# Transposing queries and decay logits before the sigmoids in a fused attention and recurrence kernel

## The reference, cut to what matters

```python
qa, ka, va, za, qr, fr, ir, zr = _project(_rmsnorm(hp, norm_g[l]), w_in[l])
...
log_f = jnp.logaddexp(jnp.log(lb), jnp.log1p(-lb) + jax.nn.log_sigmoid(fpre))
key = (1.0 - lb) * jax.nn.sigmoid(-fpre)
q = jax.nn.silu(qr.astype(f32))
...
cum = jnp.cumsum(log_f, axis=2)
...
scores = jnp.einsum('bhtsd,bhsd->bhts', decay * q[:, :, :, None, :], k)
o = jnp.einsum('bhts,bhsv->bhtv', scores, v) + jnp.einsum('bhtd,bhdv->bhtv', q * jnp.exp(cum), state)
...
o = o_attention * silu(za), o_recurrence * silu(zr), then mix @ w_out and a last rmsnorm
```

## Time and profile before

| | |
|---|---|
| runs | 1533.69, 1535.79, 1536.41 us: median 1535.79 |
| profiled execution | 1534.05 us, of which the span from first to last instruction is 1532.3 |
| PE busy | 1485.4 us, 97% of the span |
| DVE, ACT, POOL busy | 59%, 60%, 51% |
| granted clock of TensorE | 0.993 of full over the span |
| DMA | 30.9% of the 16 engines in the main queue |

### The profile page before, as it was taken

How to read it: one execution, slowest core, us unless ns; L and a number is a source line. 1 busy time by engine, 2 the same in 40 slices (tenths; PEclk the granted TensorE clock), 3 DMA queues, 4 the chain that set the end, 5 groups by cost and what they waited for, 6 DMA issues and landing times.

```text
span 1532.3 us, 25316 instructions
## 1 busy us (share of the span) xinstructions
PE 1485.4 (97%) x8296; PEld 1271.3 (83%) x8296; DVE 901.3 (59%) x2055; ACT 917.5 (60%) x2326; POOL 777.6 (51%) x1492
## 2 busy tenths in 40 slices
PE   5899999997999999999999999999999999999997
PEld 3788888886888888888888888888888888888886
DVE  5566666676555665675565656765556666632332
ACT  6677777684656666676666665866666666611111
POOL 7755655667555665476546565565544435500000
PEclk9999999999999999999999999999999999999999
DMA  8453333251542211224342221124322210244331
GB/s 261 157 182 145 124 124 114 73 150 50 149 128 90 77 60 49 69 67 126 108 126 69 70 70 44 64 72 162 126 71 70 69 67 23 99 142 147 123 123 68
DMA packets 101879, 157.50 MB, mean 103 GB/s; under 512 B 10688, under 2 KB 80192, under 8 KB 93056
## 3 DMA queue, kind: packets, MB, share of 16 engines
q1 hardware_dynamic: 101760, 156.01, 30.9%
HBM read 111.42 MB, written 44.56 MB: 102 GB/s over the span
## 4 chain that ended last, share of the span: by engine, by line
PE 86%; DVE 4%; POOL 4%; issue 2%; ACT 2%; SPq 1%; DMA 0%; POOLq 0%; DVEq 0%; ACTq 0%
PE pab L571 43%; PE oar L638 8%; PE qkb L689 7%; PE qkb L595 6%; PE qkb L753 6%; PE pab L753 6%; PE tb L629 4%; DVE scores L1155 2%; PE tb L668 2%; PE tb L740 1%; POOL w_raw L1318 1%; PE oar L611 1%; PE oar L608 1%; SPq L320 1%; PE oar L610 1%
## 5 line engine op out<-in xcount | busy, mean ns | idle before, releaser
L571 PE MATMUL pab<-w_hi,xr 128*128 128x512 f32 x2176 | 782.8, 402 | 11.7 <-ACT w_hi L809 7.9
L571 PEld LDWEIGHTS pab<-w_hi,xr 128*128 128x128 f32 x2176 | 412.0, 189 | 91.8 <-issue 9.7
L571 PE MATMUL pab<-w_lo,xr 128*128 128x512 f32 x1088 | 426.8, 392 | 0.0
L1383 POOL TENSOR_TENSOR dd<-dd 128x64 f32<-128x64 f32 x340 | 101.5, 298 | 399.1 <-DVE dd L1138 399.0
L571 PEld LDWEIGHTS pab<-w_lo,xr 128*128 128x128 f32 x1088 | 206.8, 190 | 32.7
L689 PE MATMUL qkb<-kp,q 128*128 128x512 f32 (+3 forms) x656 | 184.1, 362 | 2.9 <-DVE mxs L1155 1.6
L860 ACT ACTIVATE fb<-pab,nrs 128x256 f32<-128x256 f32 x68 | 32.2, 474 | 243.3 <-PE pab L571 243.3
L915 ACT ACTIVATE scores<-scores,nmx 128x128 f32<-128x128 f32 (+16 forms) x136 | 156.7, 1161 | 10.1 <-DVE nmx L1165 10.1
L1106 DVE TENSOR_TENSOR q<-tb,q 128x256 fp32r<-128x256 f32 x68 | 28.8, 424 | 225.5 <-ACT kp L902 225.5
L1155 DVE CUSTOM_DVE_ANT_0 scores<-qkb,bias 128x512 f32<-128x512 f32 (+4 forms) x136 | 84.9, 625 | 128.9 <-PE qkb L689 128.8
L638 PE MATMUL oar<-vv,at 128*128 128x128 f32 x1104 | 151.8, 277 | 0.3
(11 more groups left out here) (154 smaller groups left out, 2661.7 us busy)
## 6 DMA issues: line engine op xcount, KB each, us to landing
xr<-xs SPq DMA_DIRECT2D x51, 1024.0 KB, 5.2
xs<-xr SPq DMA_DIRECT2D x17, 1024.0 KB, 4.9
w_raw<-in_w_in SPq DMA_DIRECT2D x48, 256.0 KB, 6.0
w_raw<-in_x_turned SPq DMA_DIRECT2D x17, 512.0 KB, 4.5
mix<-mx SPq DMA_DIRECT2D x68, 128.0 KB, 2.2
xr<-mix SPq DMA_DIRECT2D x17, 512.0 KB, 4.9
w_raw<-in_x_prompt SPq DMA_DIRECT2D x16, 512.0 KB, 3.8
scores<-in_x_prompt SPq DMA_DIRECT2D x16, 512.0 KB, 4.2
```

The source lines that it names most:

```text
L571: last = mm(pab[:, b, :], x, w[:, kt, 512 * b:512 * b + 512], start=(kt == 0 and part == 0 and w is w_hi), stop=(kt == KT - 1 and part == 1))
L1383: g.tensor_tensor(o[:, :, 0, :], ref, c[:, :, 0, :], sub)
```

## The change

- PE transposes the plain recurrent query and decay logits (two transposes out of a new tile rq) ahead of step b = 0, kt = 2 instead of three transposed results ahead of kt = 6.
- ACT's `recurrence_columns` only copies the four column groups; a new `recurrence_sigmoids`, right behind it, makes the sigmoids from the transposed tile in PSUM, so it waits for the transposes. `copy_recurrence` becomes `log_decay` with one instruction.
- DVE makes qt out of the transposed query and the sigmoid; the factor 1 - lb of the key goes into its product with the decays.
- Levels are packed: at the five upper levels only the 64 later columns are made by POOL (in five instructions more), multiplied on PE (128x64 matmuls), masked and added (five adds in place of one reduction). The sum lands in the first 128 columns of masked, of which st is now a view.
- The weights of head 1, half b = 0, are scaled by norm_g while ACT and DVE split them; POOL's eight scalings of them in round 16 of head 0 are gone.

```diff
-                    if b == 0 and kt == 6:
+                    if b == 0 and kt == 2:
                         transpose_recurrence(h, t, first)
...
+                    if part == 0:
+                        mm(qkb[:, u % 2, 0:P], kl[:, 1, :], ql[:, 0:P], start=True, stop=True)
+                    for i, j in enumerate(levels):
+                        c0 = HP * i + (P if part == 0 else 0)
+                        late = 2 * P + HP * j
+                        last = mm(qkb[:, u % 2, c0:c0 + HP], kl[:, 2 + j, :], ql[:, late:late + HP], start=True, stop=True)
...
-                need(pe, h, "pb_free", t + 1)
-                tr(tb[:, u % 2, 0:P], nb[:, :], ident[:, :])
-                tr(tb[:, u % 2, P:2 * P], rc[:, 1, :], ident[:, :])
-                tr(tb[:, u % 2, 2 * P:3 * P], rc[:, 2, :], ident[:, :]).then_inc(S["rect_t"], 1)
+                need(pe, h, "rec_nat", t + 1)
+                for j in range(2):
+                    last = tr(tb[:, u % 2, P * j:P * j + P], rq[:, j, :], ident[:, :])
+                last.then_inc(S["rect_t"], 1)
...
+            def recurrence_sigmoids(h, t):
+                u = rec_use(h, t)
+                need(act, h, "rect_t", t + 1)
+                F(fb[:, 0:2, :].rearrange("p g c -> p (g c)"), tb[:, u % 2, 0:2 * P], ACT.Exp, scale=-1.0)
+                link(h, F(fb[:, 2, :], tb[:, u % 2, P:2 * P], ACT.Exp))
                 link(h, F(fb[:, :, :], fb[:, :, :], ACT.Ln, bias=1.0))
...
+                F(rc[:, :, :], fb[:, :, :], ACT.Exp, scale=-1.0).then_inc(S["rec_sig"], 1)
...
                     recurrence_columns(h, t)
+                    recurrence_sigmoids(h, t)
...
-                    copy_recurrence(h, t)
+                    log_decay(h, t)
...
+                    tt(masked[:, a:b], qkb[:, u % 2, 0:b - a], causal[:, a:b], ALU.mult).then_inc(S["qk_free"], 1)
+                    need(dve, h, "qk_free", u + 1)
+                    for j in levels:
+                        late = st.rearrange("p (b a r) -> p b a r", a=2, r=HALVES[j])[:, :, 1, :]
+                        level = masked[:, P + HP * j:P + HP * j + HP].rearrange("p (b r) -> p b r", r=HALVES[j])
+                        if added:
+                            need(dve, h, "level_sum", (len(HALVES) - 1) * t + added)
+                        summed = tt(late, late, level, ALU.add)
...
-                        if first:
-                            for kt in range(KT):
-                                scale_weights(h, 0, kt)
                         split_weights(h, 1, range(KT))
```

More of the change, by code:

```diff
@@ L93, in scaled_of @@
     if h == 1:
-        return (0 if b else KT) + kt + 1
-    return 2 * KT * (h - 1) + 2 * kt + (1 if b else 2)
+        return kt + 1
+    return KT + 2 * KT * (h - 2) + 2 * kt + (1 if b else 2)
 def hi_of(b, kt):
@@ L589, in rec_scores @@
                 need(pe, h, "q_decayed", t + 1)
-                for part, blocks in enumerate((range(1, 5), range(5, NS))):
+                for part, levels in enumerate(((0, 1), (2, 3, 4))):
                     u = qk_use["rec", t, part]
                     need(pe, h, "qk_free", u - 1)
[L593 to L596, removed]
+                    if part == 0:
[4 more added lines that the diff above has]
+                        last = mm(qkb[:, u % 2, c0:c0 + HP], kl[:, 2 + j, :], ql[:, late:late + HP], start=True, stop=True)
+                    last.then_inc(S["kscore_done"], 1)
                 need(pe, h, "fin_done", t)
@@ L807, in split_weights @@
                         act.wait_ge(S[f"raw_in{b}{kt}"], (h + 1) * 16 + 16)
-                    gain = gn[:, kt:kt + 1] if first else 1.0
+                    gain = gn[:, kt:kt + 1] if h + 1 < HEADS and not scaled else 1.0
                     F(w_hi[:, kt, 512 * b:512 * b + 512], raw_piece(h + 1, b, kt), ACT.Copy, scale=gain
@@ L858, in recurrence_columns @@
                 pb = pab[:, 1, :]
-                scale, minus = xrs[:, t:t + 1], nrs[:, t:t + 1]
-                F(fb[:, 0:2, :].rearrange("p g c -> p (g c)"), pb[:, 0:2 * P], ACT.Exp, scale=minus)
-                link(h, F(fb[:, 2, :], pb[:, P:2 * P], ACT.Exp, scale=scale))
-                link(h, F(fb[:, :, :], fb[:, :, :], ACT.Ln, bias=1.0))
[L863 to L867, removed]
+                F(rq[:, :, :].rearrange("p g c -> p (g c)"), pb[:, 0:2 * P], ACT.Copy, scale=xrs[:, t:t + 1]).then_inc(S["rec_nat"], 1)
+                F(vr[:, slot3(t), :], pb[:, 2 * P:3 * P], ACT.Copy, scale=xrs[:, t:t + 1])
+                need(act, h, "gates", t)
+                F(zz[:, 1, :], pb[:, 3 * P:4 * P], ACT.Copy, scale=xrs[:, t:t + 1])
+                F(ez[:, 1, :], pb[:, 3 * P:4 * P], ACT.Exp, scale=nrs[:, t:t + 1]).then_inc(S["b_evac"], 1)
+            def recurrence_sigmoids(h, t):
[3 more added lines that the diff above has]
+                link(h, F(fb[:, 2, :], tb[:, u % 2, P:2 * P], ACT.Exp))
+                link(h, F(fb[:, :, :], fb[:, :, :], ACT.Ln, bias=1.0))
+                if t > 0 or not (isinstance(h, int) and h == 0):
+                    need(act, h, "k_decayed", t)
+                F(rc[:, :, :], fb[:, :, :], ACT.Exp, scale=-1.0).then_inc(S["rec_sig"], 1)
             def gate_sigmoids(h, t):
@@ L887, in sum_squares, with log_decay @@
                 F(junk[:, P:2 * P], oar[:, 1, 0:P], ACT.Square, accum_out=ssq[:, 1:2]).then_inc(S["sumsq"], 1)
[L889 to L894, removed]
+            def log_decay(h, t):
+                need(act, h, "rec_floor", t + 1)
+                F(lf[:, :], rc[:, 1, :], ACT.Ln, scale=lbh[:, 1:2], bias=lbh[:, 0:1]).then_inc(S["log_f"], 1)
             def copy_qk(h, t):
@@ L1044, in _ @@
             for j in range(2):
-                v.tensor_tensor_reduce(out=nb[:, HD * j:HD * j + HD], in0=lamv[:, 2 * j, :], in1=lamv[:, 2 * j + 1, :], scale=1.0,
+                v.tensor_tensor_reduce(out=rq[:, 0, HD * j:HD * j + HD], in0=lamv[:, 2 * j, :], in1=lamv[:, 2 * j + 1, :], scale=1.0,
                                        scalar=0.0, op0=ALU.mult, op1=ALU.add, accum_out=lam[:, j:j + 1]
@@ L1361, in apply_decay @@
                 need(pool, h, "decay_ready", t + 1)
-                g.tensor_tensor(ql[:, :, :], qt[:, :].unsqueeze(1).to_broadcast([P, NS, P]), xx[:, NX - NS:NX, :],
-                                ALU.mult).then_inc(S["q_decayed"], 1)
+                g.tensor_tensor(ql[:, 0:2 * P].rearrange("p (l c) -> p l c", l=2),
+                                qt[:, :].unsqueeze(1).to_broadcast([P, 2, P]), xx[:, NX - 2:NX, :], ALU.mult)
+                for j, s in enumerate(HALVES):
+                    late = 2 * P + HP * j
+                    halves = [a.rearrange("p (b a r) -> p b a r", a=2, r=s)[:, :, 1, :] for a in (qt[:, :], xx[:, 2 + j, :])]
+                    last = g.tensor_tensor(ql[:, late:late + HP].rearrange("p (b r) -> p b r", r=s), *halves, ALU.mult)
+                last.then_inc(S["q_decayed"], 1)
             def head_scales(h, t, body):
```

86 lines of the change are left out of this document (44 added, 42 removed).

## The result

The changed kernel takes 1555.41 us (median of 4 runs, 1554.02 to 1556.34); the kernel before, run on the same chip, takes 1535.72 (4 runs). The ratio on record is 1.0135, 95% interval 1.0123 to 1.0146 (the two medians alone give 1.0128): slower by 1.3%. The forecast was 1553.0. The profiled execution has a span of 1554.5 against 1532.3 before, so the traces differ by 22.2 us, 2.5 more than the medians: the profiled run of the changed kernel was its slowest.

The account below looks back on a forecast made before the run. PE, busy 97% of the span, bounds the kernel, with the ACT, DVE, combine chain just under it. +30 + 3.3 + 0 - 11 - 5 = +17 on 1534.05 gives 1551, on the median's footing 1553 us; range 1530 to 1573.

Parts of the forecast that it names:

- Long rounds, +30: Rounds 9 to 16: softmax waits behind sigmoids, so PE waits for combine; 7.6 us a head, 30 for four heads.
- Short rounds, 0: Rounds 1 to 8: DVE sets the pace and eats PE's saved transpose; 0 a head, bounds -0.9 and +4.
- First rounds of heads 1 to 3, +3.3: Sigmoids come behind the gate column that waits for POOL; 1.1 us each, 3.3 together.
- Border of heads 0 and 1, -11: POOL's eight scalings go, ending PE's wait ahead of head 1's first recurrent scores; about 11 us gained, bounds 8 and 12.
- Start, -5: Fewer, narrower POOL masks come about 4 us sooner, PE stops earlier for first columns; 5 us gained, range 1 to 6.
- The forecast's +17: Whole kernel: sum of all terms, +30 + 3.3 + 0 - 11 - 5, added to the profiled execution's 1534.05 us.
- slow adds: Rival on DVE's five dependent adds: at 0.35 each, rounds 1 to 8 pay 0.5 each, 16 more, 1569 us; chance 0.12.
- Columns do not set the pace: Denies the rival that matmul width sets PE's pace: 0.56 a round off, at most 4 us gained, 1549; chance 0.05.
- The rule that the prediction weighed: PE's score matmuls: spacing is columns over 2.4 GHz plus 2.5 ns, saving 0.27 a round; prediction went by measured rows.
- The chain stays under PE: Faster rival: long rounds do not wait because the chain stays within PE's 5.94 us; 1512 us if none waits; chance 0.17.
- the 0.14 us here: Round 15 before the change: slack of PE's first softmax-weight transpose after the earliest start that combine allows, 0.14 us.

Follow-up runs that it names:

- The order run: Changed kernel with softmax ahead of the sigmoids in ACT's queue in rounds 9 to 16, transposes unmoved, DVE's columns and decay logarithm moved along: 1534.79 us, ratio 1.0004.
- the three places of the transposes: Changed kernel with only the two transposes moved: to kt = 3, 1735.8 us; to kt = 1, 1537.55 us; to kt = 0 in rounds 9 to 16, 1523.28 us.
- norm_g alone: Kernel before with only head 1's first half of weights multiplied by norm_g in the split, POOL's eight scalings gone: 1523.6 us, ratio 0.993.
- the runs with the late gates: Gates' column copies put behind the softmax: on the changed kernel 1553.32 us; on the one with early transposes in rounds 9 to 16, 1520.77 us.
- two parts of this one: Kernel before with norm_g in one split and the packed levels, without the turned layout: 1518.86 us, ratio 0.99.
- the run with the late transposes: Changed kernel with the two transposes at kt = 3 instead of kt = 2, so behind the recurrent scores too: 1735.8 us, ratio 1.1312.

## Why the prediction came out

Its steps, one by one, with what the trace of the changed kernel gives.

- *Long rounds, +30.* Right in mechanism and size. From the first transpose to PE's L634 the chain is 969.85 to 977.08, 7.23 (worked out: 7.28); the softmax starts 1.99 behind the transpose (2.02). The rounds 9 to 15 lose 6.4 to 6.7 a head (6.1), round 16 of head 1 loses 1.46 (1.5). Four heads: 26.2, and 4 times 1.5, that is 32; the round 16 of the heads 0 and 3 can't be read alone, since the border and the last stage follow them. The order run shows that the queue is the cause, and the three places of the transposes that it is the time of the sigmoids that counts.
- *Short rounds, 0.* Slightly too pessimistic. In round 6 of head 3 of the changed kernel, against the earlier trace rows:

```profile
1114.61 0.38 PE L665 MATMUL tb<-ident,rq 128*128 128x128 f32 x2
...
1120.34 0.82 PE L634 MATMUL tb<-ident,scores 128*128 128x128 f32 x6
...
1116.72 0.23 DVE L1133 TENSOR_SCALAR rc<-rc 128x128 f32<-128x128 f32 x1 [2.76 <-ACT rc L879]
1117.06 0.41 DVE L1101 TENSOR_TENSOR masked<-qkb,causal 128x256 f32<-128x256 f32 x1
...
1119.41 1.15 DVE L1196 SCALAR_TENSOR_TENSOR scores<-scores,cneg 128x512 f32<-128x512 f32 x2
```

  The floor starts 2.11 after the transpose (2.15). From the mask to `combine` it takes 2.35, where 2.05 for the sums and 0.44 for the two small instructions had been taken. So PE keeps the saved transpose: rounds 1 to 8 of heads 1 to 3 win 1.25 each, 3.7 together, a little outside the bound of 0.9 a head.
- *First rounds of heads 1 to 3, +3.3.* 1.03 in head 2, 0.58 in head 3, and some 0.7 in head 1: 2.3.
- *Border of heads 0 and 1, -11.* Rounds 16 and 0 together get 8.8 shorter; with the 1.46 and 0.7 that the points above put on them the gain is 10.9. The scores of head 1's first round follow without a wait. norm_g alone gives 10.5.
- *Start, -5.* **This term was mis-sized.** Round 2 of head 0 begins at 61.5 instead of 62.1: 0.6, under the bound of 1. The masks took 7.25 us, 2.4 less than 9.65, where 4 less had been taken (last section). And PE stops longer for the first columns, 8.6 in the list of waits; the kernel before had, in its list:

```profile
PE tb L659 <- DVE nb L1118: 6.2, 1, 6.2
```

  In the profiled runs of kernels with the same first rounds this point scatters from 59.6 to 62.1, so the term's true size stays open by some 2 us. And what is won there is asked back: in rounds 2 and 3 of head 0 the sigmoids, behind the gates' copies, wait for POOL, +1.4 together, which the runs with the late gates take away (15.25 and 15.63). That scatters too: in the order run, with the same first rounds, these two take 15.25 and 15.66, and round 4 pays instead, 17.33 for 16.39. The prediction had seen that wait in the first rounds of heads alone.
- *Not in the sum.* Round 16 of head 2 lost another 1.6 to the granted clock (last section).

Together, in the traces: +26.2 (rounds 9 to 15) + 1.5 + 1.6 + 1.6 (round 16 of heads 1 and 2, its clock) + 1.6 (first rounds of heads 2 and 3) - 3.7 - 8.8 (border) - 0.6 (start) + 0.6 (rounds 2 to 8 of head 0: +1.4 - 0.8) + 2.3 (from round 16 of head 3 to the end) = +22.3, against the 22.2 of the spans. The forecast's +17 was nearly right because its large terms were, and in part by luck: the 4.5 us that the short rounds won unforeseen (3.7 and 0.8) stand against 2 more in the long rounds, 1.6 of the clock and 1.4 of the gates. The start's missing 4 us make up most of the difference.

Of the rivals, slow adds are out: two adds take 0.48 and three 0.75 in round 15, 0.24 to 0.25 each, as taken. Columns do not set the pace either: from the first of ten matmuls of 64 columns to the start of what follows it is 1.07 us (970.29 to 971.36), 0.107 each, where 128 columns took 0.11. That rival's "at most 4 us" was wrongly summed: sixteen rounds at its own 0.56 would be 9, and 1544. The rule that the prediction weighed (the Trainium skill, TensorE: Matmul & The Clock Gate, Back-to-back issue gap) would give 0.029 each, an estimate from 64 columns over 2.4 GHz plus 2.5 ns. The section gives that formula for a lone matmul and says itself that it counts too little where each brings a weight load; the measurement decides against it for these matmuls. Each of them has a load of 128 columns:

```profile
970.18 1.20 PEld L600 LDWEIGHTS qkb<-kq 128*128 128x128 f32 x10
```

One load is recorded with 0.19 us, so the ten start 0.112 apart. The Trainium skill's same page, section LDWEIGHTS (loading the stationary operand), has a weight load of 128 columns last their number over 1.2, an estimate of 0.107 us here: the spacing of the loads comes near it, their recorded length does not. That the load sets the pace was not tried by itself. "The chain stays under PE" was the one rival with weight; it came near to true with the transposes two steps earlier in the long rounds: 1523 us, with 13.7 us of PE's waits for `combine` left of 34.2.

## What to carry to other kernels

An engine that waits for nobody can still be late by what stands ahead in its queue: when a step is moved to read another engine's result, look at every instruction behind it, and ask how much slack each has, as with the 0.14 us here. A change of several parts is worth taking apart: two parts of this one win 1%, and the third costs 2.4% on top of them at one place in the program and 0.3% with its transposes two steps earlier in the long rounds. Moving an issue by "one step" means past everything that is issued at that step.

## What the runs showed of the hardware

A wait of PE can cost twice. In round 16 PE waits 2.6 us for `combine` in heads 1 and 2 alike; behind it the granted clock is 1.00 in the one and 0.50, the level of 1.2 GHz, in the other (stretches of the changed kernel, columns as above):

```profile
676.90:679.40 2.50, 2.50 (x25) 2.50 (x24) 2.50 (x5) 2.50 (x7) 1.10 (x2) 1.00 0.08 20
1004.90:1007.40 2.50, 2.50 (x14) 2.50 (x13) 2.50 (x5) 1.77 (x5) 1.09 (x2) 0.50 0.05 13
```

PE's timeline in both places, the same work behind the same wait:

```profile
674.84 1.29 PE L634 MATMUL tb<-ident,scores 128*128 128x128 f32 x8 [2.59 <-DVE scores L1196]
...
676.64 1.06 PE L643 MATMUL oar<-vv,at 128*128 128x128 f32 x8
```

```profile
1002.84 1.29 PE L634 MATMUL tb<-ident,scores 128*128 128x128 f32 x8 [2.60 <-DVE scores L1196]
...
1004.93 1.91 PE L643 MATMUL oar<-vv,at 128*128 128x128 f32 x8
```

Eight matmuls take 1.91 instead of 1.06, and the round is 1.6 longer. In the run with the late transposes, which has 67 such waits, the granted clock is 0.954 over the span, where the changed kernel has 0.991, and PE's busy time is 60.8 us longer. What decides whether the clock falls after a given wait stays open.

POOL's mask instructions took two different times for the same work. The twelve of the changed kernel, ten of them on 64 columns, took 7.25 us in its profiled run, 0.60 each, against 0.57 for the seventeen of the earlier trace rows; the ten alone are recorded with 0.55 each, and so they are in two of the runs above (the late transposes, the order alone). In the seven others that have them they took 0.31 to 0.36 each, and all twelve 4.9 to 5.4 us. Why they differ was not tried.
